# First attention of a two-block transformer kernel: the transposes of a step issued in front of its quarter of the product with V

## What is computed

```python
def global_attention(q, k, v):
    ...
    def one_block(qi):
        s = jnp.einsum('bqkgd,bskd->bkgqs', qi, k).astype(jnp.float32) * scale
        p = jax.nn.softmax(s, axis=-1).astype(v.dtype)
        return jnp.einsum('bkgqs,bskd->bqkgd', p, v)
    ...
def window_attention(q, k, v, sink):
    ...
    s = jnp.where(valid[None, :, None, None], s, -jnp.inf)
    m = jnp.maximum(jnp.max(s, axis=-1, keepdims=True), sink_l)
    e = jnp.exp(s - m)
    den = jnp.sum(e, axis=-1, keepdims=True) + jnp.exp(sink_l - m)
    p = (e / den).astype(v.dtype)
    o = jnp.einsum('bnkgqc,bnckd->bnqkgd', p, vb)
```

## Time and profile before

| | us |
|---|---|
| median of three runs | 1463.94 |
| the profiled execution, its time | 1462.92 |
| its span, first to last instruction | 1461.2 |
| TensorE busy in it | 1393.8 |
| VectorE busy in it | 684.3 |
| ScalarE busy in it | 541.2 |
| attention of the first block: start of step 0's scores to the first product behind the last quarter | 111.8 to 244.0 |

### The profile page before, as it was taken

The page is one execution under the profiler, slowest core; times in us unless marked ns, Lnnn a source line. Parts: engine busy times, 40 slices in busy tenths (PEclk is TensorE's granted clock), DMA queues, the critical chain, the costliest instruction groups (busy, mean ns, idle before and its releaser), DMA issues.

```text
span 1461.2 us, 14901 instructions
## 1 busy us (share of the span) xinstructions
PE 1393.8 (95%) x6182; PEld 1097.6 (75%) x6182; DVE 684.3 (47%) x893; ACT 541.2 (37%) x717; POOL 145.7 (10%) x132
## 2 busy tenths in 40 slices
PE   6788999999999999998999999899999999999995
PEld 5564466877888888886787777688888888888874
DVE  5777665455444443225433543465345445423345
ACT  5346655544233233224223444734323223222232
POOL 3252011330000000002000000002000000001012
PEclk9999999999999999998999999999999999999997
DMA  6110000203232222332222110223222322233311
GB/s 228 58 58 29 1 1 30 90 26 116 87 115 87 89 94 81 98 99 93 87 87 87 58 58 8 87 87 115 87 87 91 112 87 99 76 100 99 115 60 58
DMA packets 20291, 117.76 MB, mean 81 GB/s; under 512 B 2432, under 2 KB 3072, under 8 KB 9472
## 3 DMA queue, kind: packets, MB, share of 16 engines
q1 hardware_dynamic: 19088, 114.57, 22.7%
q10 hardware_dynamic: 1136, 2.24, 0.4%
HBM read 114.70 MB, written 2.10 MB: 80 GB/s over the span
## 4 chain that ended last, share of the span: by engine, by line
PE 89%; DVE 6%; ACT 2%; DMA 1%; issue 1%; POOLq 0%; POOL 0%; DVEq 0%; SPq 0%
PE ps L431 87%; PE ps L611 2%; DVE w_lo L1136 1%; DMA w_raw<-weights 1%; DVE rt L1143 1%; ACT w_hi L777 1%; DVE X L1136 0%; DVE ps L1143 0%; ACT rt L777 0%; DVE rt L1136 0%; DVE OUT L1143 0%; DVE h_lo L1143 0%; DVE nmax L1293 0%; DVE F L1140 0%; DVE hf L1136 0%
## 5 line engine op out<-in xcount | busy, mean ns | idle before, releaser
L431 PE MATMUL ps<-h_hi,w_hi 128*128 128x512 f32 x1248 | 497.9, 399 | 30.7 <-DVE w_lo L1136 13.6
L431 PE MATMUL ps<-h_lo,w_hi 128*128 128x512 f32 x1248 | 489.3, 392 | 0.0
L431 PE MATMUL ps<-h_hi,w_lo 128*128 128x512 f32 x1248 | 489.2, 392 | 0.0
L1136 DVE TENSOR_TENSOR w_lo<-w_raw,w_hi 128x2048 fp32r<-128x2048 f32 (+2 forms) x116 | 241.9, 2088 | 257.4 <-ACT w_hi L777 257.3
L431 PEld LDWEIGHTS ps<-h_hi,w_hi 128*128 128x128 f32 x1248 | 236.8, 190 | 89.1 <-issue 20.3
L777 ACT ACTIVATE w_hi<-w_raw 128x2048 fp32r<-128x2048 f32 (+2 forms) x116 | 201.5, 1738 | 201.3 <-DMA w_raw<-weights 201.2
L431 PEld LDWEIGHTS ps<-h_lo,w_hi 128*128 128x128 f32 x1248 | 236.7, 190 | 50.5 <-issue 2.7
L431 PEld LDWEIGHTS ps<-h_hi,w_lo 128*128 128x128 f32 x1248 | 236.3, 189 | 50.5
L375 POOL TENSOR_TENSOR sqsum<-sqsum,sq 128x512 f32<-128x512 f32 x62 | 94.5, 1525 | 922.4 <-ACT sq L777 920.6
L431 PE MATMUL ps<-mid_hi,w_hi 128*128 128x512 f32 x352 | 136.9, 389 | 0.0
L431 PE MATMUL ps<-mid_lo,w_hi 128*128 128x512 f32 x352 | 136.9, 389 | 0.0
(11 more groups left out here) (164 smaller groups left out, 1239.3 us busy)
## 6 DMA issues: line engine op xcount, KB each, us to landing
w_raw<-weights SPq DMA_DIRECT2D x82, 1024.0 KB, 4.9
w_raw<-weights SPq DMA_DIRECT2D x32, 704.0 KB, 4.1
X<-x_t SPq DMA_DIRECT2D x4, 512.0 KB, 9.2
out_t<-OUT SPq DMA_DIRECT2D x8, 256.0 KB, 2.0
c<-constants ACTq DMA_DIRECT2D x1, 1280.0 KB, 8.6
wp_raw<-weights SPq DMA_DIRECT2D x1, 1024.0 KB, 4.8
hf<-p_t ACTq DMA_DIRECT2D x1, 512.0 KB, 3.7
w_raw<-weights SPq DMA_DIRECT2D x2, 128.0 KB, 2.3
```

The source lines that it names most:

```text
L431: return nc.tensor.matmul(out, lhsT, rhs, start=start, stop=stop, skip_group_check=loose)
L1136: return nc.vector.tensor_tensor(out, a, b, op)
```

## The change

Two lines of TensorE's program move down by one place. The quarter of the product with V is issued behind the transposes of its step instead of in front of them. Everything else, also the order within VectorE's and ScalarE's programs, the banks and the semaphores, is as before.

```diff
             for s, (kind, h, b, k0, k1) in enumerate(STEPS):
                 scores(s + 2)
-                if s >= 6:
-                    weighted((s - 6) // 4, (s - 6) % 4)
                 if s in LATE_STEPS:
                     item(LATE_STEPS[s])
                 pe.wait_ge(pn_ready, s + 1)
...
                     last = nc.tensor.transpose(ps[:, 3 + s % 2, (kb - k0) * P:(kb - k0 + 1) * P],
                                                prob[:, s % 3, (kb - k0) * P:(kb - k0 + 1) * P], ident[:, :])
                 last.then_inc(tr_done, 1)
+                if s >= 6:
+                    weighted((s - 6) // 4, (s - 6) % 4)
                 if s == NORM_A_STEP + 4:
                     total(n_group_a)
```

## The result

The launch takes 1476.11 us, the median of six runs (1469.49 to 1478.75), against 1462.61 before (six runs, 1460.55 to 1464.51). The ratio is 1.0088, 95% interval 1.0065 to 1.0111: slower, as forecast, but by twice the size (13.5 us instead of 6.45) and just outside the range. The profiled execution took 1476.45 us, its span is 1474.7.

A forecast was written before the change was run, and what follows sets the result against it. The attention was taken as bound by TensorE's own work, except for a few waits for VectorE. Order 2.8, first copies 1.5, rotary embedding 1.05 and group norm 1.1 sum to +6.45 us: 1470.4 us, range 1465.7 to 1474.8.

The forecast's parts named there:

- order, global steps: Plain global attention steps: changed neighbours of scores, transposes and quarter cost +0.05 us a step, 2.05 becoming 2.10.
- order, windowed steps: Windowed attention steps, costed like the global ones: +0.05 us a step from changed neighbours.
- first copy of a head, global: Steps 10 to 30, every fourth: transposes wait 0.25 us for ScalarE's PT copy, +1.5 us in all.
- first copy, windowed: From step 34 on: the PT copy taken as hidden, costing nothing; otherwise 0.25 us in 7 more steps.
- rotary embedding, step 8: Step 8: TensorE waits 1.3 us for VectorE's late scaling, with the quarter still to follow; +1.05 us.
- group norm: Steps 48 to 53: VectorE, nearly full, gets scores 0.8 us later and the quarter follows the wait; +1.1 us.
- Item 1: Each step: scores followed by transposes take 0.55 us, followed by a quarter 0.64; saves 0.09.
- item 2: Each step: four transposes last 0.60 us behind scores, 0.66 behind a quarter; saves 0.06.
- rival of windowed steps that lose more: Windowed steps' scores and copies don't give what was assumed: 2.7 + 1.75 us on top, 1474.8 us; chance 0.04.
- The clock: Rival: TensorE's clock falls once more behind step 8's new wait, losing 1.75 us, 1472.2 us; chance 0.08.
- rival of an order that costs nothing: Whole attention: the order itself is free and only waits cost, +3.65 us, 1467.6 us; chance 0.22.
- faster rival: Weight loads of quarter and scores become hidden, saving 0.15 us in 56 steps; 1459.2 us with waits; chance 0.04.

The follow-up runs named there:

- e7: Kernel before, each quarter using V's 128 columns of both key heads to fill the array's width, attention's values left out; 1452.28 us, one run.
- e8: Changed kernel's order (quarter behind the transposes) with full-width quarters, attention's values left out; 1462.77 us, one run.
- e11: Changed kernel with the quarter in front of the transposes again in step 8 alone; 1473.08 us, ratio 1.006 against the kernel before.
- e9: Kernel before with V between zeros, so full-width quarters compute the right values and both heads accumulate in one bank; 1453.83 us, ratio 0.9938.
- e2: Kernel before with the quarter behind the transposes in the windowed steps 32 to 63 only; 1473.06 us, ratio 1.0068.

## Why the prediction was right or wrong

The direction and the mechanisms were right: plain steps that cost more through the change of width, waits for the copy, behind the rotary embedding and in the group norm; the only other wait is a short one in step 40. Two windowed terms, mis-sized, hold most of what the sum missed. The terms, in us, against the stretch's 10.09 (the predicted 6.45 also counts steps 6 and 7, 0.10, which lie ahead of the stretch):

| term | predicted | measured |
|---|---|---|
| order, global steps | 1.2 | 1.1 |
| order, windowed steps | 1.6 | 3.15 |
| first copy of a head, global | 1.5 | 2.2 |
| first copy, windowed | 0 | 0.75 |
| rotary embedding, step 8 | 1.05 | 1.1 |
| step 40 | not seen | 0.33 |
| group norm | 1.1 | 1.26 |
| the end | 0 | 0.22 |

- **Order in global steps.** Predicted 2.10, measured 2.10 (164.96 to 167.06), each piece within 0.01 us. The first weight load of the scores starts with its product, as named among the signs. e7 and e8 show the cause.
- **Order in windowed steps: mis-sized, the largest error.** I costed them like the global ones, +0.05; they cost +0.10. Before, step 31 is 0.86 for scores, mask and sink, 1.00, and 0.41:

```profile
180.37 0.59 PE L431 MATMUL ps<-KB,QB 128*128 128x384 f32 x2
...
180.97 0.33 PE L431 MATMUL ps<-gain,ident 128*128 128x1 f32 x2
181.23 1.07 PE L431 MATMUL ps<-PT,VA 128*64 128x512 f32 x2
182.23 0.66 PE L611 MATMUL ps<-ident,F 128*128 128x128 f32 x4
182.64 0.59 PE L431 MATMUL ps<-KB,QB 128*128 128x384 f32 x2
```

After it is 0.81, 0.56 and 1.00:

```profile
187.06 0.61 PE L431 MATMUL ps<-KB,QB 128*128 128x384 f32 x2
...
187.68 0.33 PE L431 MATMUL ps<-gain,ident 128*128 128x1 f32 x2
187.87 0.63 PE L609 MATMUL ps<-ident,F 128*128 128x128 f32 x4
188.43 1.07 PE L431 MATMUL ps<-PT,VA 128*64 128x512 f32 x2
189.43 0.44 PE L431 MATMUL ps<-KB,QB 128*128 128x384 f32 x1
```

  Item 1 saves 0.07 here (0.26 from the sink product to the next, then 0.19), not 0.09, and item 2 saves 0.03, not 0.06: the four transposes last 0.63 behind the one-column sink product, 0.60 in global steps. Their first weight load, 0.14 us long, starts 0.11 ahead of its product there and 0.23 ahead in a global step, which leaves the 0.03 unhidden. The same 0.63 stands in e8, so it isn't the width. The prediction named this gap and bounded it at 2.7 more; 1.6 came. Its rival of windowed steps that lose more came nearest to what the stretch shows (10.9 us against 10.1), and I had given it a chance of 0.04.
- **First copy: mis-sized by two small terms.** The copy starts 1.16 behind the quarter's start, as predicted, and ends at 167.82; the transposes start at 167.97, 0.15 behind it. I had taken 0.06, from a pair of VectorE and TensorE. And transposes that had to wait take 0.56 until the quarter, not 0.53. 0.37 instead of 0.25, six times.

```profile
167.22 0.60 ACT L777 ACTIVATE PT<-ps 128x512 f32<-128x512 f32 x1 [2.09 <-PE ps L431]
```

  In the windowed steps I took it as hidden; it shows every fourth step with about 0.1 (the step of the copy grows by 0.20 instead of 0.10). 0.1 is too short for the trace to list as a wait.
- **Rotary embedding.** The wait is 1.20, the loss 1.15 with the order's 0.05. Right, down to the piece; that 0.41 of it can't be had back by step 8 alone is e11's.

```profile
136.63 0.66 PE L609 MATMUL ps<-ident,F 128*128 128x128 f32 x4 [1.20 <-DVE F L1140]
...
138.22 0.73 PE L431 MATMUL ps<-KA,QA 128*128 128x512 f32 x2
```

- **Group norm.** The wait that I expected near 215, now at 224.24, is 0.75 us. The other, at 225.03 before, is split over steps 52 and 53. Steps 48 to 53 together cost 1.26 beyond the order, 1.1 predicted.

```profile
224.24 0.44 PE L609 MATMUL ps<-ident,F 128*128 128x128 f32 x2 [0.75 <-DVE F L1140]
...
233.30 0.44 PE L609 MATMUL ps<-ident,F 128*128 128x128 f32 x2 [0.54 <-DVE F L1140]
235.55 0.55 PE L609 MATMUL ps<-ident,F 128*128 128x128 f32 x3 [0.36 <-DVE F L1140]
```

- **Step 40: not seen.** VectorE's scaling takes 1.14 us there instead of 0.35 while GpSimd adds squares, and the transposes of step 40 wait. It ends 0.16 us behind GpSimd's addition (206.91 and 206.75), as if held until that was over. The same happens in step 41, whose 0.09 is in the windowed row of the table. Both scalings were as long before, 1.17 and 1.22 us, but then a quarter stood in front of the transposes.

```profile
205.48 1.27 POOL L375 TENSOR_TENSOR sqsum<-sqsum,sq 128x512 f32<-128x512 f32 x1 [65.43 <-ACT sq L777]
...
205.77 1.14 DVE L1140 TENSOR_SCALAR F<-F,rden 128x256 f32<-128x256 f32 x1
...
206.96 0.44 PE L609 MATMUL ps<-ident,F 128*128 128x128 f32 x2 [0.15 <-DVE F L1140]
```

- **The end.** Step 62's transposes wait 0.62 us for the copy, and 0.22 is left of it, where I had entered 0.
- **The clock: a rival that was right in kind and put in the wrong place.** I gave it 0.08, as one fall behind step 8, and there the clock stayed up. In some launches it is low for long in the norm's steps instead. Over twelve launches the lower mean clock goes with 1.9 us of the 12.6. How much of that lies in the norm's steps isn't shown: the profile of the changed kernel itself has none there.
- **The waits in all.** I had expected 5 to 7 us instead of 3.5. Counted from 118 us and without step 0's, they are 7.0.
- The rival of an order that costs nothing falls with e8: without a change of width it costs nothing in the global steps, with it 4 us over the stretch. The faster rival falls with the rows above.

So the steps of the prediction that failed are the costing of the windowed steps like the global ones (1.6 predicted, 3.15 measured) and the first copies (1.5 for the global ones and nothing for the windowed ones, 2.2 and 0.75 measured), together 3.0 of the 3.7 us that the stretch has over the sum. The attention's own 10.1 alone, on the six-run median of before, would have given 1472.7 us, inside the range. What carried the result over its upper end are 1.9 us that go with the clock, which the sum had at nothing, and 1.5 of the median difference (0.6 of the mean) that remain unassigned; six runs of a kernel that spread over 9 us allow as much.

## What to carry to other kernels

An order written by hand has its slack in what stands in front of a wait; moving independent work from there to behind the wait costs at every place where the producer is late, also where no wait is listed now. So list the producer's late steps (extra work on its engine, an engine beside it that slows it, a copy that depends on the moved work itself) before moving. And where a narrow product alternates with full-width ones, ask first whether it can be filled up with zeros: that was worth 10 us here (e9), more than any order tried.

## What the runs showed of the hardware that was not expected

- A product with 64 output rows between full-width ones costs 0.30 us a step more than the same columns at full width (2.05 against 1.75). Its weight load and the one behind it start with their products; at full width the quarter's starts 0.22 us ahead.
- TensorE's start behind the end of a ScalarE copy was 0.15 us, at 167.97 and again at 251.78; behind VectorE it was 0.06.
- A mean clock of 0.976 or less was granted in 12 of 36 launches with one order of eleven steps, and in none of 96 with the other. In the seven profiles with a low stretch there, it starts at the end of 16 one-column products or up to 1.5 us behind it, and while it lasts the profile shows TensorE busy all the time (17.10 of 17.10 us in e2).
- VectorE's scaling of 256 columns took 1.14 us instead of 0.35 beside GpSimd's addition, and ended 0.16 us behind it.
